# Causal mask by GpSimd selects, diagonal key tiles first, and a re-planned instruction order in a decoder layer on eight cores

## The chip, the cores and the metric

One Trainium2 chip, eight cores, one launch. Each core computes one batch element of the layer; the cores exchange nothing and share the weights in HBM. The time is the device time in microseconds of the slowest core, the median of several runs. Five engines of a core matter here: TensorE (PE, matmuls into PSUM), VectorE (DVE), ScalarE (ACT), GpSimd (POOL, which also issues the DMAs that cast to bf16) and SyncE (SP, which issues the other DMAs). Each runs its own instructions strictly in the order in which the program lists them, and waits at semaphores.

## The reference

```python
h = rmsnorm(x, norm_mix_pre)
proj = h @ w_in                                  # q, k, v, u; 2048 tokens x 1024
q, k = rope(q), rope(k)
y_attn = moba_attention(q, k, v)                 # 8 heads x 64
y_pool = pool_mixer(u, w_pool, b_pool, pool_scale)
x = x + rmsnorm(concat([y_attn, y_pool]) @ w_out, norm_mix_post)
h = rmsnorm(x, norm_ffn_pre)
x = x + rmsnorm(conv_ffn(h, w_up, conv_w, conv_b, w_down), norm_ffn_post)   # D_FF 2816
```

In `moba_attention` a query sees its own block of 256 keys, causally, and the three fully past blocks with the highest gate scores. Inside the own block, scores of keys later than the query are replaced by a very negative number before the softmax; their weights are therefore zero.

## The kernel before

Tokens are cut into 16 tiles of 128 and 4 groups G of 512. The program has three parts.

**Projections.** Tiles of x are loaded, normalised (`prep_norm`: a square with a row sum on ACT or DVE at L619, L620, L629; two small POOL instructions at L604 and L606; a scaling at L635 or L636) and transposed: tiles 0 to 7 by PE (L650), tiles 8 to 15 by a transposing DMA. `vu1` (L769) makes v and u, `qk_unit` (L674) makes q and k of four heads and rotates them on DVE (L681) and POOL (L687, L689); a DMA then moves the halves into place. Weights arrive as float32 in staging slots and are cast by ACT (L551) or DVE (L549). The slots 4 and 5 lie in the same memory as the four x buffers `xs0` to `xs3`, so an x tile can be loaded there only when the weights of that slot have been cast. At the start 88 matmuls on zeros (L491) keep PE running.

**Attention** (`attn(G)`, L818). For each head h and key tile kt up to the group's last, a score matmul puts 128 keys x up to 512 queries into a PSUM bank (L830), ACT takes the exponential into one of eight bf16 buffers `PT` (L844), and for each query tile of 128 a matmul with V (L848, 65 columns, the last one the row sum) adds into the head's bank. The MoBA mask of whole blocks is part of the score matmul (8 extra rows of its 72). The last four key tiles of a group lie on the diagonal; there a second score matmul (L835, identity times a triangle of -30000) adds the causal mask to one 128 x 128 square before the exponential. DVE divides by the row sum (L863, L865). There are three score banks and one bank for the sums, so the sums of the next head wait for the division of this one.

**Output projection and FFN.** `sec1` (L904) multiplies by w_out, with a square (L911), two small POOL instructions, a scaling (L914), the residual add on POOL (L917), a second square, a scaling (L922) and a transposing DMA; tiles 0 to 11 are woven into `attn(2)` and `attn(3)`. `up_section` (L954) and `down` (L1072) are the FFN, twice.

**What sets the order.** Nothing of the order is written by hand. A planner (`Sched.schedule`) plays all instructions through with a cost for each (`cost`, `LAT`, `SLACK`) and a priority (`sc.base`), and lists for each engine the instructions in the order in which they come up; small random amounts (`SEED`, `SHAKE`) are added to the ends, so that another seed gives another order. The waits that the program then contains are true dependencies. What the planner's costs get wrong, an engine pays by waiting in its fixed order.

Of the kernel before, what the change touches and what calls it, by code (L numbers as in the profile page):

```python
# [17 lines left out]
H = 8  # L18
# [3 lines left out]
NEG = -30000.0  # L22
# [3 lines left out]
WARM = 88  # L26
SEED, SHAKE = 923, 0.15
PE_Y = 3
# [41 lines left out]
class Sched:  # L70
# [9 lines left out]
    def __init__(self, nc, st):  # L80
        self.nc = nc
        self.st = st
        self.streams = {e: [] for e in COMPUTE + ("sp",)}
        self.sems = {e: st.enter_context(nc.semaphore("s_" + e)) for e in COMPUTE}
        self.dsem = {}
        self.ops = []
        self.order = 0
        self.base = 0
        self.rng = np.random.default_rng(SEED)

    def _collect(self, eng, rd, wr, wp, deps):
# [11 lines left out]
    def _add(self, o, raw, rd, wr, wp, prio=None):  # L103
        o["shake"] = SHAKE * float(self.rng.random()) if "pe" not in o["alts"] else 0.0
        seen = set()
# [54 lines left out]

    def dma(self, queue, key, pairs, rd=(), wr=(), wp=(), deps=(), nbytes=524288, cast=False, prio=None, turn=False):
        raw = self._collect(queue, rd, wr, wp, deps)
        if key not in self.dsem:
            self.dsem[key] = [self.st.enter_context(self.nc.semaphore("d_" + key)), 0]
        fn = lambda e: [e.dma_start_transpose(out=o_, in_=i_) if turn else e.dma_start(out=o_, in_=i_) for (o_, i_) in pairs]  # L165
        o = dict(kind="dma", key=key, turn=turn, sig=False, seq=0, slack=0.0, ndma=len(pairs), nbytes=nbytes, cast=cast,
                 alts={queue: (fn, (0.62 if queue == "pool" else 0.45) * len(pairs), 0.0)})
        return self._add(o, raw, rd, wr, wp, prio)

    def schedule(self):  # L170
# [26 lines left out]
        while done < len(ops):  # L197
# [15 lines left out]
            t, _, e = best  # L213
# [43 lines left out]
            else:  # L257
                fin = t + o["dur"]
            o["t0"], o["t1"] = t, fin
            fin += o["shake"]  # L260
# [91 lines left out]
def build():  # L352
# [26 lines left out]
    with ExitStack() as st:  # L379
# [124 lines left out]

        def load_x(tt, deps=()):
            s = tt % 4
            dma("sp", "fx%d" % s, [(xs[s], x_d[tt * 128:(tt + 1) * 128, :])], wr=[buf("xs%d" % s)], deps=deps)

# [5 lines left out]
        for tt in range(NT):  # L514
            xsrc[tt] = (xs[tt % 4], buf("xs%d" % (tt % 4)))
        for i in range(3):
# [107 lines left out]
        def prep_norm(tt):  # L624
# [6 lines left out]
            else:  # L631
# [5 lines left out]
                1024, dict(dve="x2", act="sb"), rd=[xab, rb], wr=[xb])  # L637
            if tt == 3:
                scaled.append(xb.w[-1])
# [178 lines left out]
        def attn(G, between=None):  # L818
            nkt = 4 * G + 4
            its = [(h, kt) for h in range(H) for kt in range(nkt)]  # L820
            N = len(its)
# [3 lines left out]
            def qk(n):  # L825
# [4 lines left out]
                last_sc[0:] = [op("pe", lambda e: e.matmul(bk[u.ids[0]][:, c0:512], lhsT=KT[kt // 4][0:72, h, (kt % 4) * 128:(kt % 4) * 128 + 128],  # L830
                                            rhs=QT[G % 2][0:72, h, c0:512], start=True, stop=(nd < 0)),
                   rd=[buf("KT%d_%d" % (kt // 4, h // 4)), buf("QT%d_%d" % (G % 2, h // 4)),
                       buf("QTm%d" % (G % 2)), buf("KTind%d" % (kt // 4))], wr=u.b, n=512 - c0, deps=last_sc[:])]
                if nd >= 0:
                    op("pe", lambda e: e.matmul(bk[u.ids[0]][:, c0:c0 + 128], lhsT=ident, rhs=tri, start=False, stop=True),  # L835
                       rd=[buf("cst")], wp=u.b, n=128)

            qk(0)
            qk(1)
            for n in range(N):  # L840
# [4 lines left out]
                                                                  scale=SCALE),  # L845
                   rd=u.b, wr=[buf("PT%d" % p)], n=512 - c0)
                for qb in range(c0 // 128, 4):
                    op("pe", lambda e, h=h, kt=kt, qb=qb, p=p, pb=pb: e.matmul(  # L848
                        bk[pb.ids[0]][:, qb * 65:qb * 65 + 65], lhsT=PT[p][:, qb * 128:qb * 128 + 128], rhs=VA[:, kt, h, 0:65],
                        start=(kt == 0 and qb == 0), stop=(kt == nkt - 1)),  # L850
                       rd=[buf("PT%d" % p), VA_b[kt], buf("VAones%d" % (kt // 8))], n=64, **W(kt == 0 and qb == 0, pb.b[0]))
                if n + 2 < N:
                    qk(n + 2)
                if kt == nkt - 1 and between is not None:
                    between(h)
                if kt == nkt - 1:
                    r, k = h % 2, (h // 2) % 2
# [254 lines left out]
        def next_x(G):  # L1112
            for tt in range(4 * G, 4 * G + 4):
                load_x(tt, bulk if G < 3 else move1)
            load_rope(G, bulk)
# [33 lines left out]
        lw = buf("ws%d" % wslot[7]).w[-1]  # L1149
        bulk.append(lw)  # L1150
        vu(0, 0)
# [24 lines left out]
        qk_some(1, (("k", 0), ("q", 0), ("k", 1), ("q", 1)))  # L1176
        move1 = union(["QT1_1", "KT1_1"])
        sc.base = P_ATT
        attn(0)
# [85 lines left out]
def host_prep(inputs):  # L1265
# [52 lines left out]
    idtri[:, 0, :] = np.eye(128)  # L1318
    idtri[:, 1, :] = np.where(tp > t, NEG, 0.0)
    c = lambda a: np.ascontiguousarray(a, dtype=f)  # L1320
# [18 lines left out]
```

How the kernel before makes its waits and increments, by code:

```python
            def body(e):  # L322
                waited = {}
                for o in self.streams[eng]:
                    need = {}
                    for d in o["deps"]:
                        k = "d_" + d["key"] if d["kind"] == "dma" else d["eng"]
                        if k not in need or need[k][1] < d["seq"]:
                            need[k] = (d["sem"], d["seq"])
                    for k, (sem, val) in need.items():
                        if waited.get(k, 0) < val:
                            e.wait_ge(sem, val)
                            waited[k] = val
                    ins = o["fn"](e)
                    if o["kind"] == "dma":
                        for i in ins:
                            i.then_inc(o["sem"], 16)
                    elif o["sig"]:
                        ins.then_inc(o["sem"], 1)
```

## Time and profile before

| | |
|---|---|
| median of 3 runs | 779.73 us (776.73, 779.73, 795.33) |
| the profiled execution | 778.17 us, span of its slowest core 776.6 us |
| spans of the eight cores | 768.8 to 776.6 us, mean granted clock 0.988 to 0.995 |
| busy PE, DVE, ACT, POOL | 754.9, 469.2, 387.4, 286.7 us |
| PE waits that the profile names | 14.1 us in 8 waits, the longest 5.9 us |

A span runs from the first to the last instruction of the slowest core; the 1.6 us between it and the execution's time lie around it. "Busy" for PE is modelled and includes the pipeline's latency, so the pace of matmuls is read from their starts. A name in an arrow such as `L848 <- DVE L865` says which line waited and which line's end released it.

### The profile page before, as it was taken

What the parts mean: (1) busy time and instruction counts of PE and PEld (TensorE: products, weight loads), DVE (VectorE), ACT (ScalarE), POOL (GpSimd) and SP (SyncE); (2) the same over time, 40 slices, a digit from 0 to 9 for tenths busy, and PEclk for the clock granted to TensorE, in tenths of its full rate; (3) what the DMA queues carried; (4) which work ended last, traced back from release to release, by engine and by line L of the source; (5) the groups of instructions that cost most, each with busy time, mean ns of one, the idle gap of its engine ahead of it and who ended that gap; (6) DMA issues with size and microseconds to landing.
All of it is one profiled execution on the core that took longest, in us unless ns stands there. A gap on an engine that the chain in (4) does not pass through costs nothing.

```text
span 776.6 us, 14872 instructions; the slowest of 8 cores (768.8 to 776.6 us)
## 1 busy us (share of the span) xinstructions
PE 754.9 (97%) x4866; PEld 385.0 (50%) x4866; DVE 469.2 (60%) x702; ACT 387.4 (50%) x619; POOL 286.7 (37%) x309
## 2 busy tenths in 40 slices
PE   7997999999999999999999999999999999999996
PEld 5644655455655555444444444444444444444443
DVE  4786658654555555578787781322877877772223
ACT  3835567158899999554554440211445454441111
POOL 1273324301455560557655562100343444321000
PEclk9899899999999999999999999999999999999998
DMA  8978589119579565678897676342444444001321
GB/s 256 321 243 199 81 187 198 50 28 144 108 193 215 161 170 131 109 136 160 169 194 122 116 115 102 106 166 108 109 82 82 69 71 79 1 0 57 110 99 62
DMA packets 63067, 99.21 MB, mean 128 GB/s; under 512 B 35856, under 2 KB 41872, under 8 KB 61968
## 3 DMA queue, kind: packets, MB, share of 16 engines
q1 hardware_dynamic: 50304, 65.88, 31.2%
q0 software_dynamic: 12688, 32.38, 25.6%
q8 instruction: 41, 0.67, 0.4%
q14 instruction: 34, 0.28, 0.1%
HBM read 100.60 MB, written 16.78 MB: 151 GB/s over the span
## 4 chain that ended last, share of the span: by engine, by line
PE 90%; DMA 3%; DVE 2%; issue 2%; ACT 1%; POOL 1%; SPq 1%; DVEq 0%; ACTq 0%; POOLq 0%
PE ps L954 38%; PE ps L1072 18%; PE ps L830 7%; PE ps L904 7%; PE ps L769 7%; PE ps L674 5%; PE ps L848 4%; DMA MEM<-x 3%; PE ps L1065 1%; PE ps L835 1%; SPq L165 1%; PE ps L797 1%; ACT MEM L844 0%; PE ps L650 0%; DVE MEM L681 0%
## 5 line engine op out<-in xcount | busy, mean ns | idle before, releaser
L954 PE MATMUL ps<-MEM 128*128 128x512 bf16 x1408 | 309.8, 379 | 1.3 <-DVE MEM L975 1.3
L954 PEld LDWEIGHTS ps<-MEM 128*128 128x128 bf16 x1408 | 136.5, 98 | 164.0 <-issue 2.2
L965 ACT ACTIVATE MEM<-ps,MEM 128x1024 f32<-128x1024 f32 x88 | 105.9, 1203 | 147.2 <-PE ps L954 144.0
L844 ACT ACTIVATE MEM<-ps 128x512 bf16<-128x512 f32 (+1 forms) x320 | 149.4, 541 | 38.7 <-PE ps L835 17.1
L991 POOL TENSOR_TENSOR MEM<-MEM 128x1024 bf16<-128x1024 f32 x44 | 105.2, 2391 | 118.9 <-DVE MEM L978 82.0
L968 DVE SCALAR_TENSOR_TENSOR MEM<-ps,MEM 128x1023 f32<-128x1023 f32 x88 | 112.8, 1282 | 57.9 <-ACT MEM L965 57.7
L1072 PE MATMUL ps<-MEM 128*128 128x512 bf16 x660 | 142.8, 379 | 0.0
L971 DVE SCALAR_TENSOR_TENSOR MEM<-ps,MEM 128x1022 f32<-128x1022 f32 x88 | 112.7, 1281 | 8.2 <-DVE MEM L968 0.5
L1072 PEld LDWEIGHTS ps<-MEM 128*128 128x128 bf16 x660 | 64.4, 98 | 78.0
L830 PE MATMUL ps<-MEM 72*128 72x512 bf16 (+1 forms) x320 | 102.8, 349 | 0.1
L604 POOL TENSOR_SCALAR MEM<-MEM 128x1 f32<-128x1 f32 x63 | 13.7, 218 | 197.7 <-ACT MEM L1077 118.8
L1081 DVE SCALAR_TENSOR_TENSOR MEM<-ps,MEM 128x1024 f32<-128x1024 f32 x15 | 19.3, 1284 | 104.7 <-POOL MEM L606 104.6
L848 PEld LDWEIGHTS ps<-MEM 128*128 128x128 bf16 x1088 | 58.8, 97 | 38.4 <-issue 8.2
L1077 ACT ACTIVATE MEM<-ps 128x1024 f32<-128x1024 f32 x15 | 15.3, 1023 | 123.9 <-PE ps L1072 119.9
L848 PE MATMUL ps<-MEM 128*128 128x65 bf16 x1088 | 69.5, 193 | 6.9 <-DVE MEM L865 6.8
L904 PE MATMUL ps<-MEM 128*128 128x512 bf16 x256 | 72.9, 379 | 0.0
L769 PE MATMUL ps<-MEM 128*128 128x512 bf16 (+1 forms) x320 | 72.2, 350 | 0.1
L674 PE MATMUL ps<-MEM 128*128 128x512 bf16 x256 | 58.2, 379 | 0.0
L165 POOL DMA_DIRECT2D MEM<-w_up_r x44 | 26.1, 594 | 71.4 <-PE ps L954 33.7
L989 ACT ACTIVATE MEM<-MEM 128x1024 f32<-128x1024 f32 x44 | 46.1, 1048 | 4.7 <-DVE MEM L971 3.2
L917 POOL TENSOR_TENSOR MEM<-MEM 128x1024 f32<-128x1024 f32 x16 | 43.2, 2699 | 13.5 <-DVE MEM L914 13.4
L681 DVE TENSOR_TENSOR MEM<-ps,MEM 128x512 f32<-128x512 f32 x64 | 42.4, 685 | 6.6 <-PE ps L674 4.7
(103 smaller groups left out, 620.6 us busy)
## 6 DMA issues: line engine op xcount, KB each, us to landing
MEM<-w_up_r POOLq DMA_DIRECT2D x44, 512.0 KB, 5.5
MEM<-x SPq DMA_DIRECT2D x32, 512.0 KB, 5.5
x1s<-MEM SPq DMA_DIRECT2D x16, 512.0 KB, 5.4
MEM<-x1s SPq DMA_DIRECT2D x16, 512.0 KB, 3.9
out<-MEM SPq DMA_DIRECT2D x15, 512.0 KB, 2.6
MEM<-w_down POOLq DMA_DIRECT2D x22, 256.0 KB, 7.5
MEM<-w_qk SPq DMA_DIRECT2D x4, 1024.0 KB, 20.7
MEM<-MEM SPq DMA_DIRECT2D x24, 128.0 KB, 5.6
```

Of the source, the lines that this page charges most:

```text
L674: mm = op("pe", lambda e, c=c, s=s: e.matmul(bk[bb[s].ids[0]], lhsT=wqk[wi][:, c, s * 128:(s + 1) * 128], rhs=HY[:, c, G * 512:(G + 1) * 5 ...
L769: op("pe", lambda e, c=c, ca=ca, cb=cb: e.matmul(bk[u.ids[0]][:, ca:cb], lhsT=HY[:, c, tt * 128:(tt + 1) * 128], rhs=wvu[s][:, c, ca:cb], ...
L830: last_sc[0:] = [op("pe", lambda e: e.matmul(bk[u.ids[0]][:, c0:512], lhsT=KT[kt // 4][0:72, h, (kt % 4) * 128:(kt % 4) * 128 + 128], rhs= ...
L844: op("act", lambda e, c0=c0, u=u, p=p: e.activation(out=PT[p][:, c0:512], in_=bk[u.ids[0]][:, c0:512], func=AF.Exp, scale=SCALE), rd=u.b, ...
L848: op("pe", lambda e, h=h, kt=kt, qb=qb, p=p, pb=pb: e.matmul(bk[pb.ids[0]][:, qb * 65:qb * 65 + 65], lhsT=PT[p][:, qb * 128:qb * 128 + 128 ...
L904: mm = op("pe", lambda e, c=c, dh=dh: e.matmul(ps(u)[:, dh * 512:(dh + 1) * 512], lhsT=HY[:, c, tt * 128:(tt + 1) * 128], rhs=w_out_sb[:, ...
L954: mm = op("pe", lambda e, c=c, half=half, pr=pr, ws=ws, tb=tb: e.matmul(bk[pr.ids[tb]], lhsT=wu[ws][:, c, half * 128:(half + 1) * 128], rh ...
L965: op("act", lambda e, pr=pr, ch=ch, ts=ts: e.activation(out=tA[ts], in_=ps(pr)[:, :], func=AF.Identity, scale=cwb[:, ch, 2:3], bias=cwb[:, ...
L968: op("dve", lambda e, pr=pr, ch=ch, ts=ts: e.scalar_tensor_tensor(out=tA[ts][:, 1:1024], in0=ps(pr)[:, 0:1023], scalar=cwb[:, ch, 1:2], in ...
L971: op("dve", lambda e, pr=pr, ch=ch, ts=ts: e.scalar_tensor_tensor(out=tA[ts][:, 2:1024], in0=ps(pr)[:, 0:1022], scalar=cwb[:, ch, 0:1], in ...
L991: op("pool", lambda e: e.tensor_tensor(out=gbuf[p], in0=tA[tg], in1=tA[tv], op=ALU.mult), rd=[tA_b[tg], tA_b[tv]], wr=[g_b[p]], deps=alias ...
L1072: op("pe", lambda e, c=c, dh=dh, i=i, p=p: e.matmul(bk[p.ids[dh]], lhsT=gbuf[c][:, i * 128:(i + 1) * 128], rhs=wd[c][:, dh * 512:(dh + 1) ...
```

## The change

Five things are edited.

1. The second score matmul goes. After the exponential of a diagonal tile, POOL sets the 128 x 128 square above the diagonal to zero in `PT` by an `affine_select`. Only the one matmul with V that reads this square waits for POOL (buffer `PM`); the others wait for ACT alone, as before.
2. In a head the four diagonal key tiles come first, then the earlier ones.
3. x tiles 8 to 15 use the x buffers in another rotation (tile 8 goes to `xs2` and not to `xs0`), and their loads no longer wait for the last staged weight (`bulk`).
4. The casts of the first weight wait for the scaling of x tile 1 and not of tile 3.
5. The planner takes x loads to land 3 us later than its costs say, and draws its random amounts from other seeds, twice as large; the second seed begins at `attn(0)`. The constant `tri` is changed on the host, and nothing reads it any more.

```diff
-SEED, SHAKE = 923, 0.15
+SEED, SHAKE = 1348, 0.3
+SEED2, SHAKE2 = 1506, 0.3
+X_LATE = 3.0
...
             else:
                 fin = t + o["dur"]
+            fin += o.get("late", 0.0)
...
-        def load_x(tt, deps=()):
-            s = tt % 4
-            dma("sp", "fx%d" % s, [(xs[s], x_d[tt * 128:(tt + 1) * 128, :])], wr=[buf("xs%d" % s)], deps=deps)
+        def load_x(tt, deps=(), turn=0):
+            s = (tt + turn) % 4
+            dma("sp", "fx%d" % s, [(xs[s], x_d[tt * 128:(tt + 1) * 128, :])], wr=[buf("xs%d" % s)], deps=deps, late=X_LATE)
...
-            if tt == 3:
+            if tt == 1:
                 scaled.append(xb.w[-1])
...
-            its = [(h, kt) for h in range(H) for kt in range(nkt)]
+            kts = list(range(4 * G, nkt)) + list(range(4 * G))
+            its = [(h, kt) for h in range(H) for kt in kts]
...
-                                            rhs=QT[G % 2][0:72, h, c0:512], start=True, stop=(nd < 0)),
+                                            rhs=QT[G % 2][0:72, h, c0:512], start=True, stop=True),
...
-                if nd >= 0:
-                    op("pe", lambda e: e.matmul(bk[u.ids[0]][:, c0:c0 + 128], lhsT=ident, rhs=tri, start=False, stop=True),
-                       rd=[buf("cst")], wp=u.b, n=128)
...
+                nd = kt - 4 * G
+                if nd >= 0:
+                    o = op("pool", None, rd=[buf("PT%d" % p), buf("cst")], wr=[buf("PM%d" % p)])
+                    keep = lambda e, c0=c0, p=p: e.affine_select(out=PT[p][:, c0:c0 + 128], in_=PT[p][:, c0:c0 + 128], pattern=[[1, 128]],
+                                                                 compare_op=ALU.is_ge, fill=0.0, base=0, channel_multiplier=-1)
+                    o["alts"] = dict(pool=(keep, 0.34, 0.38))
                 for qb in range(c0 // 128, 4):
...
-                        start=(kt == 0 and qb == 0), stop=(kt == nkt - 1)),
-                       rd=[buf("PT%d" % p), VA_b[kt], buf("VAones%d" % (kt // 8))], n=64, **W(kt == 0 and qb == 0, pb.b[0]))
+                        start=(kt == kts[0] and qb == 0), stop=(kt == kts[-1] and qb == 3)),
+                       rd=[buf("PT%d" % p), VA_b[kt], buf("VAones%d" % (kt // 8))] + ([buf("PM%d" % p)] if qb == nd else []),
+                       n=64, **W(kt == kts[0] and qb == 0, pb.b[0]))
...
-                load_x(tt, bulk if G < 3 else move1)
+                load_x(tt, bulk if G < 3 else move1, 2)
...
         lw = buf("ws%d" % wslot[7]).w[-1]
-        bulk.append(lw)
...
+        sc.rng, sc.amp = np.random.default_rng(SEED2), SHAKE2
         sc.base = P_ATT
         attn(0)
```

The lines of the changed kernel lie 3 to 9 further down (L165 becomes L168, L491 L495, L650 L654, L769 L773, L830 L835, L844 L846, L848 L856, L865 L874, L917 L926; the select is L852). The order is changed throughout; three places follow.

**SP, after the loads of the staged weights** (w_ut are the last two of them; `x` are tiles 8 to 11, `MEM 32x4x512` the halves of k and q after the rotation, whose wait for `s_pool` is one for the POOL rotation of group 1). Before:

```order
L165 DMA MEM<-w_ut 128x2048 [waits d_ws4,s_act,s_dve]
L165 DMA MEM<-MEM 32x4x512 [waits d_ws0,s_pool]
L165 DMA MEM<-poolc 128x768 [waits d_ws4]
L165 DMA MEM<-x 128x1024 [waits d_ws5,s_act,s_dve]
L165 DMA MEM<-MEM 32x4x512 [waits s_pool]
L165 DMA MEM<-x 128x1024
L165 DMA MEM<-x 128x1024 [waits s_dve,s_act]
L165 DMA MEM<-x 128x1024
```

Now:

```order
L168 DMA MEM<-w_ut 128x2048 [waits d_ws4,s_act,s_dve]
L168 DMA MEM<-x 128x1024 [waits d_ws5,s_act,s_dve]
L168 DMA MEM<-x 128x1024
L168 DMA MEM<-rope 128x1024 [waits d_rp0,s_dve]
L168 DMA MEM<-poolc 128x768 [waits d_ws4]
L168 DMA MEM<-MEM 32x4x512 [waits d_ws0,s_pool]
L168 DMA MEM<-x 128x1024 [waits s_dve,s_act]
L168 DMA MEM<-x 128x1024
```

Tiles 8 and 9 now stand ahead of the first DMA that waits for POOL; tiles 10 and 11 still stand behind it.

**POOL, in `attn(3)`** (small instructions of the norms and the residual adds of `sec1`, whose wait for `s_dve` is the scaling before). Before:

```order
L917 TENSOR_TENSOR MEM<-MEM 128x1024 [waits d_fx1,s_dve]
L604 TENSOR_SCALAR MEM<-MEM 128x1 [waits s_act]
L606 TENSOR_TENSOR MEM<-MEM 128x1 [waits s_pool]
L604 TENSOR_SCALAR MEM<-MEM 128x1 [waits s_dve]
L606 TENSOR_TENSOR MEM<-MEM 128x1 [waits s_pool]
L917 TENSOR_TENSOR MEM<-MEM 128x1024 [waits d_fx2,s_dve]
```

Now:

```order
L926 TENSOR_TENSOR MEM<-MEM 128x1024 [waits d_fx0,s_dve]
L852 AFFINE_SELECT MEM<-MEM 128x128 [waits s_act,s_pe] x4
L608 TENSOR_SCALAR MEM<-MEM 128x1 [waits s_act]
L608 TENSOR_SCALAR MEM<-MEM 128x1 [waits s_dve]
L610 TENSOR_TENSOR MEM<-MEM 128x1 [waits s_pool] x2
L926 TENSOR_TENSOR MEM<-MEM 128x1024 [waits d_fx1,s_dve]
L852 AFFINE_SELECT MEM<-MEM 128x128 [waits s_act,s_pe] x2
```

The four selects of a head stand behind residual adds that wait for DVE and for a load.

**PE, at the start** (L491, now L495, are the matmuls on zeros; L650, now L654, the transposes of x tiles; L769, now L773, the v and u matmuls). Before:

```order
L491 MATMUL ps<-MEM 128x256 x15
L650 MATMUL ps<-MEM 128x128 x8
L491 MATMUL ps<-MEM 128x256 x14
L650 MATMUL ps<-MEM 128x128 x16
L769 MATMUL ps<-MEM 128x256 x48
```

Now:

```order
L654 MATMUL ps<-MEM 128x128 x8
L495 MATMUL ps<-MEM 128x256 x4
L773 MATMUL ps<-MEM 128x256 x3
L495 MATMUL ps<-MEM 128x256
L773 MATMUL ps<-MEM 128x256 x2
L495 MATMUL ps<-MEM 128x256 x2
L773 MATMUL ps<-MEM 128x256 x7
L495 MATMUL ps<-MEM 128x256
L773 MATMUL ps<-MEM 128x256 x4
L495 MATMUL ps<-MEM 128x256 x5
L654 MATMUL ps<-MEM 128x128 x16
L773 MATMUL ps<-MEM 128x256 x48
```

Sixteen of the v and u matmuls now come between the matmuls on zeros, ahead of the transposes of tiles 2 and 3.

## Rows read from the trace of the kernel before

**Rows 1.** The page: span, and section 1, busy us (share of the span) xinstructions:

```profile
span 776.6 us, 14872 instructions; the slowest of 8 cores (768.8 to 776.6 us)
...
PE 754.9 (97%) x4866; PEld 385.0 (50%) x4866; DVE 469.2 (60%) x702; ACT 387.4 (50%) x619; POOL 286.7 (37%) x309
```

**Rows 2.** Stretches: length, busy us PE, PEld, DVE, ACT, POOL, clock, DMA share, GB/s:

```profile
20.60:72.10 51.50, 51.46 (x367) 30.37 (x365) 41.18 (x87) 33.26 (x69) 26.50 (x33) 0.97 0.87 257
72.10:78.10 6.00, 0.06 (x2) 0.05 (x2) 1.74 (x4) 0.00 (x0) 0.19 (x1) 0.77 0.81 204
78.10:82.10 4.00, 4.00 (x27) 2.92 (x28) 2.92 (x6) 3.49 (x7) 2.54 (x4) 0.50 0.18 43
82.10:186.00 103.90, 102.86 (x916) 58.09 (x915) 64.27 (x183) 57.54 (x118) 31.82 (x34) 1.00 0.62 114
186.00:317.00 131.00, 128.90 (x1329) 75.55 (x1325) 69.02 (x97) 118.87 (x240) 58.59 (x70) 1.00 0.70 160
317.00:760.00 443.00, 442.94 (x2053) 200.41 (x2054) 273.11 (x292) 163.25 (x166) 162.90 (x153) 1.00 0.49 102
```

**Rows 3.** Timeline, PE, around 71 us: start, length, instruction:

```profile
71.42 0.22 PE L835 MATMUL ps<-MEM 128*128 128x128 bf16 x1
71.48 0.27 PE L830 MATMUL ps<-MEM 72*128 72x256 bf16 x1
71.59 0.22 PE L835 MATMUL ps<-MEM 128*128 128x128 bf16 x1
```

**Rows 4.** Groups of instructions by shape: count, busy us, mean ns, idle before:

```profile
L844 ACT ACTIVATE MEM<-ps 128x512 bf16<-128x512 f32 x224 | 119.3, 606 | 23.9 <-PE ps L830 10.0 <-PE ps L848 6.7 <-PE ps L835 5.6
...
L835 PE MATMUL ps<-MEM 128*128 128x128 bf16 x128 | 27.8, 221 | 0.0
...
L844 ACT ACTIVATE MEM<-ps 128x128 bf16<-128x128 f32 x32 | 9.1, 284 | 13.7 <-PE ps L835 10.7 <-PE ps L830 2.5
```

**Rows 5.** Timeline, PE, 72 to 82 us: in brackets the idle time before:

```profile
78.08 0.71 PE L848 MATMUL ps<-MEM 128*128 128x65 bf16 x10 [5.94 <-DVE MEM L865]
78.60 2.32 PE L769 MATMUL ps<-MEM 128*128 128x256 bf16 x10
```

**Rows 6.** Timeline, DVE, 65 to 80 us:

```profile
76.36 1.23 DVE L620 SCALAR_TENSOR_TENSOR MEM<-MEM 128x1024 bf16<-128x1024 f32 x1 [6.52 <-DMA MEM<-x]
...
77.51 0.42 DVE L865 TENSOR_TENSOR MEM<-ps,MEM 128x256 bf16<-128x256 f32 x1
```

**Rows 7.** Timeline, SP, 38 to 75 us:

```profile
59.75 0.70 SPq L165 DMA_DIRECT2D MEM<-MEM  x1
...
61.25 0.33 SPq L165 DMA_DIRECT2D MEM<-x  x1
...
62.28 2.00 SPq L165 DMA_DIRECT2D MEM<-x  x3
```

**Rows 8.** Waits of the SP queue, 40 to 70 us: total, times, longest:

```profile
SPq L332 <- POOL MEM L687: 15.6, 2, 15.4
```

**Rows 9.** A stretch of two microseconds, columns as in Rows 2:

```profile
56.00:58.00 2.00, 2.00 (x11) 0.89 (x10) 2.00 (x4) 0.00 (x0) 2.00 (x3) 1.00 0.00 0
```

**Rows 10.** Timeline, PE, 14 to 45 us:

```profile
17.74 1.01 PE L650 MATMUL ps<-MEM 128*128 128x128 bf16 x8 [2.70 <-DVE MEM L635]
...
20.59 7.13 PE L769 MATMUL ps<-MEM 128*128 128x256 bf16 x48
```

**Rows 11.** Timeline, ACT, 38 to 48 us:

```profile
39.70 2.10 ACT L551 ACTIVATE MEM<-MEM 128x256 bf16<-128x256 f32 x5 [1.50 <-DMA MEM<-w_qk]
...
45.64 2.10 ACT L551 ACTIVATE MEM<-MEM 128x256 bf16<-128x256 f32 x5
```

**Rows 12.** One line on POOL, the small factor: duration in ns min/median/max:

```profile
L604 POOL TENSOR_SCALAR MEM<-MEM x63: 181/190/1232, 6.8 to 761.3; 128x1 f32<-128x1 f32 x63
```

**Rows 13.** One line on POOL, the residual add: duration in ns min/median/max:

```profile
L917 POOL TENSOR_TENSOR MEM<-MEM x16: 2347/2378/3266, 202.1 to 384.3; 128x1024 f32<-128x1024 f32 x16
```

**Rows 14.** One line on DVE, both tensors read from SBUF, likewise:

```profile
L922 DVE SCALAR_TENSOR_TENSOR MEM<-MEM x16: 1275/1277/2537, 208.9 to 392.5; 128x1024 bf16<-128x1024 f32 x16
```

More of the change, by code:

```diff
@@ L89, in __init__ @@
         self.rng = np.random.default_rng(SEED)
+        self.amp = SHAKE
     def _collect(self, eng, rd, wr, wp, deps):
@@ L103, in _add @@
     def _add(self, o, raw, rd, wr, wp, prio=None):
-        o["shake"] = SHAKE * float(self.rng.random()) if "pe" not in o["alts"] else 0.0
+        o["shake"] = self.amp * float(self.rng.random()) if "pe" not in o["alts"] else 0.0
         seen = set()
@@ L159, in either, with dma @@
         return o
-    def dma(self, queue, key, pairs, rd=(), wr=(), wp=(), deps=(), nbytes=524288, cast=False, prio=None, turn=False):
+    def dma(self, queue, key, pairs, rd=(), wr=(), wp=(), deps=(), nbytes=524288, cast=False, prio=None, turn=False, late=0.0):
         raw = self._collect(queue, rd, wr, wp, deps)
@@ L165, in dma @@
         fn = lambda e: [e.dma_start_transpose(out=o_, in_=i_) if turn else e.dma_start(out=o_, in_=i_) for (o_, i_) in pairs]
-        o = dict(kind="dma", key=key, turn=turn, sig=False, seq=0, slack=0.0, ndma=len(pairs), nbytes=nbytes, cast=cast,
+        o = dict(kind="dma", key=key, turn=turn, sig=False, seq=0, slack=0.0, late=late, ndma=len(pairs), nbytes=nbytes, cast=cast,
                  alts={queue: (fn, (0.62 if queue == "pool" else 0.45) * len(pairs), 0.0)})
@@ L514, in build @@
         for tt in range(NT):
-            xsrc[tt] = (xs[tt % 4], buf("xs%d" % (tt % 4)))
+            xsrc[tt] = (xs[(tt + 2 * (tt > 7)) % 4], buf("xs%d" % ((tt + 2 * (tt > 7)) % 4)))
         for i in range(3):
@@ L849, in attn @@
                         bk[pb.ids[0]][:, qb * 65:qb * 65 + 65], lhsT=PT[p][:, qb * 128:qb * 128 + 128], rhs=VA[:, kt, h, 0:65],
-                        start=(kt == 0 and qb == 0), stop=(kt == nkt - 1)),
-                       rd=[buf("PT%d" % p), VA_b[kt], buf("VAones%d" % (kt // 8))], n=64, **W(kt == 0 and qb == 0, pb.b[0]))
+                        start=(kt == kts[0] and qb == 0), stop=(kt == kts[-1] and qb == 3)),
+                       rd=[buf("PT%d" % p), VA_b[kt], buf("VAones%d" % (kt // 8))] + ([buf("PM%d" % p)] if qb == nd else []),
+                       n=64, **W(kt == kts[0] and qb == 0, pb.b[0]))
                 if n + 2 < N:
                     qk(n + 2)
-                if kt == nkt - 1 and between is not None:
+                if kt == kts[-1] and between is not None:
                     between(h)
-                if kt == nkt - 1:
+                if kt == kts[-1]:
                     r, k = h % 2, (h // 2) % 2
@@ L1318, in host_prep @@
     idtri[:, 0, :] = np.eye(128)
-    idtri[:, 1, :] = np.where(tp > t, NEG, 0.0)
+    idtri[:, 1, :] = np.where(tp > t, 0.0, 3e38)
     c = lambda a: np.ascontiguousarray(a, dtype=f)
```

## The prediction

> **What bounds the kernel now.** First the page's busy times: PE is busy 754.9 of 776.6 us [rows 1], so time is won only where PE gets less work, a better clock or fewer waits. Second the stretches [rows 2], in which the reader should compare the first two busy numbers with the length. From 317 to 760 us, in the FFN, PE is busy 442.9 of 443.0 us at full clock, and nothing of the change reaches it. From 82 to 186 and from 186 to 317 us, where the attention of the later groups lies, PE misses 1.0 and 2.1 us. The hole is at 72.1 to 78.1 us: 6 us in which PE, ACT and POOL do next to nothing, and behind it 4 us at a granted clock of 0.50, the lower of its two levels, 1.2 GHz.
>
> Third the cause of the hole, from PE backwards. PE waits 5.94 us at L848 for the division L865 of the head before [rows 5]. DVE had not come to that division, because ahead of it in its order stands the square of x tile 8 or 9, which waits 6.52 us for the load of x [rows 6]. That load was issued at 61.25 us or later [rows 7]. SP had stood 15.4 us until then for the rotation on POOL (L687) [rows 8], with the x loads queued behind a small DMA that needs it, while the DMA engines moved nothing between 56 and 58 us [rows 9]. So the hole is an x load issued late, not a shortage of bandwidth.
>
> The sum is made against the profiled execution, 778.2 us, whose slowest span is 776.6 us [rows 1]. It lies 1.6 us below the median of the runs shown, 779.7, which of three values is the middle one.
>
> **The second score matmul.** All 128 go [rows 4]. Their listed 221 ns contain the pipeline; the pace is read from starts: a matmul of 256 columns is followed after 0.11 us, and one L835 of 128 columns after 0.06 [rows 3], so 0.055 us each. 128 x 0.055 = **7.0 us** of PE. Half of them lie in the groups 2 and 3. There ACT is next: between 186 and 317 us it is busy 118.9 of 131 us, PE 128.9 [rows 2]; less 3.5 us PE still has 125.4, so PE stays the bound and the gain passes through. The exponentials also lose a predecessor, which costs or gains nothing, as they are not the bound.
>
> **The hole.** The loads of tiles 8 and 9 now stand ahead of the DMA for which SP waited 15.4 us. They need only the casts of the weights in their memory; the last ACT casts before 50 us end at 47.7 [rows 11]. Issued at about 49 us they have the idle DMA engines of 56 to 58 us [rows 9] and land at about 60, where before the square got its data at 76.4 [rows 6]. The square still stands ahead of the fourth head's division in DVE's order, but its data is then there before the 72.1 us at which PE began to wait. The wait goes, **5.9 us**, and with it the low clock, which followed the idle stretch: 4.0 us at half speed [rows 2], **2.0 us**. What is late next are tiles 10 and 11, still behind POOL; their data is wanted later, by ACT.
>
> **The start.** 16 matmuls of v and u, of 48 that took 7.13 us [rows 10], move ahead of the transposes of tile 2, for which PE waited 2.70 us. At 0.149 us each that is 2.4 us; if the clock then stays up and the other 32 run at 0.11 us, 7.13 - 3.5 = 3.6 us. Against it, weights land when they did: ACT stood 1.50 us for w_qk at 39.7 us [rows 11], and PE cannot pass that by much. DVE is busy 41.2 of the 51.5 us from 20.6 on [rows 2], so it too has little to give. Ends 0 and 3.6; I take **1.5 us**, nearer the lower end because of that wait.
>
> **The selects.** The trace has none. On POOL, one input of one column took 0.190 us (median) [rows 12]; two inputs of 1,024 columns took 2.378 [rows 13], so two of 128 columns about 0.190 + 127 x 2.19/1,023 = 0.46. The select reads one input of 128 columns; between 0.19 and 0.46 I take the middle, 0.33, since neither row is nearer. 128 x 0.33 = 42 us of POOL, which costs nothing by itself: in groups 2 and 3 it adds 21 us to 58.6 of 131 [rows 2]. What it can cost is a wait of PE. The four squares of a head come one after the other, and their matmuls with V now wait for POOL; behind them in PE's order stand the next scores. The cover is the other PE work woven in, L904 and the projections, and the fact that the matmuls of a new head wait for the division of the old one anyway. Lower end 0. Upper end: selects at 0.46 make a head's four 0.52 us late; 32 heads, half of it uncovered, 8 us. I take **2 us**, near the lower end, because PE waited only 2.1 us in 131 with ACT as its supplier [rows 2].
>
> **Diagonal tiles first** makes the last exponential of a head 606 instead of 284 ns [rows 4], 0.32 us later per head. PE's woven-in work hides it; without that cover 32 x 0.32 = 10 us. The planner's assumption on x loads, its seeds and the constant cost nothing of their own; what they move is contained above.
>
> **The sum:** 778.2 - 7.0 - 5.9 - 2.0 - 1.5 + 2.0 = 763.8, so **764 us**, with its own ends 759 (start at 3.6, no new waits: 759.7) and 769 (start at 0, new waits at 6).
>
> **Rivals.** (1) **Selects held up by DVE, 770 us.** For it: on POOL the one-column instruction took up to 1.232 us, 1.04 above its median [rows 12], the residual add up to 3.266 against 2.378 [rows 13], and on DVE the scaling L922 up to 2.537 against 1.277 [rows 14]. If every second head is held once, 16 x 1.04 = 16.6 us, half of it hidden, 8.3 us in place of the 2 in the sum: 770. Against it: the medians lie at the minima, so most instructions are not held. (The Trainium skill, "SBUF — State Buffer", section "Who interferes with whom", has a rule for this: a DVE instruction with two SBUF inputs contends with a GpSimd instruction that reads SBUF, and the second one fully blocks. The long maxima agree with that; no row shows which instruction held which.)
>
> (2) **The hole comes back elsewhere, 772 us.** Tiles 10 and 11 still wait behind POOL, and POOL now has selects ahead of the rotations that free SP. If their squares or transposes stop ACT or SP as tile 8's stopped DVE, the 7.9 us are not won: 771.7. Against it: they have two tiles' work more time than tile 8 had.
>
> (3) **The score matmuls of groups 2 and 3 pay nothing, 767 us**, as ACT, busy 91% there [rows 2], sets the pace after all: the sum less its 3.5 us. This is the way in which the change would not do what it says.
>
> (4) **Slower, 799 us: PE waits behind the residual adds.** In `attn(2)` and `attn(3)` selects stand behind a residual add of 2.38 us [rows 13] that waits in turn for a DVE scaling of about 1.28 [rows 14]: up to 3.66 us for a head, and as there is one bank for the sums, the next head cannot go on. Over 16 heads the 14.4 us won are used up at 0.9 us a head, and the kernel is over 2% slower from 1.9 us a head on, (14.4 + 15.6)/16. At 2.2 us, 60% of the most, it takes 764 + 35 = 799. Against it: before, DVE and ACT waited for these same adds without holding PE, and POOL would be busy only 80 of 131 us.
>
> **How the numbers follow.** Forecast 0.64, rival 1 0.14, rival 2 0.09, rival 3 0.05, rival 4 0.08. A range of 758 to 774 takes in the forecast's ends and rivals 1 to 3, and leaves out rival 4 and a tenth more at the edges. A measurement of this kernel tells about 2% from no change, here 764.1 us. The forecast lies at that bound; its low half and a little more, 0.42, counts as faster by over 2%. Its upper part, 0.22, and rivals 1 to 3, 0.28, make 0.50 within 2%, and rival 4 makes 0.08 slower.
>
> **What the changed profile would show.** PE's stretches without a hole near 70 us, with clock 1.00 from there on; SP's x loads issued before 52 us; 4,738 PE matmuls instead of 4,866; PE waits for L852 of under 3 us in total; POOL busy about 329 us; the FFN's stretch as long as before, some 14 us earlier. I am wrong if PE's waits for POOL exceed 6 us, if a wait for x or for a transposing DMA of x shows on PE, DVE or ACT between 55 and 110 us that reaches PE, or if the first v and u matmuls wait for their weight so long that the 64 end no earlier.

## The result, and the profile after

The changed kernel takes 769.1 us (median of four executions, three of them at 766.6 to 769.6) and the kernel before, on the same chip, 778.8: a ratio of 0.987, 95% interval 0.983 to 0.991. That is 1.3% faster, less than the 2% that the prediction wanted for "faster", and inside its range, 5 us above the forecast of 764. The fourth execution took 830.9 us, with a granted clock of 0.89 to 0.93 on four of its cores, and is left out of the ratio. The profiled execution took 768.6 us, 9.5 less than the one before, where the sum had 14.4.

The page of the changed kernel, as in [rows 1]:

```profile
span 767.1 us, 15225 instructions; the slowest of 8 cores (763.0 to 767.1 us)
...
PE 748.9 (98%) x4738; PEld 378.6 (49%) x4738; DVE 476.5 (62%) x702; ACT 387.2 (50%) x619; POOL 334.9 (44%) x437
```

PE lost its 128 matmuls (4,866 to 4,738) and 6.0 us of busy time, not 7.0 or more. GpSimd is at 334.9 us; 329 were expected. The stretches, with the columns of [rows 2]; the lines of the code have moved by 3 to 9:

```profile
72.10:78.10 6.00, 5.98 (x52) 4.00 (x50) 1.78 (x4) 5.54 (x16) 3.13 (x11) 1.00 0.73 134
78.10:82.10 4.00, 4.00 (x20) 1.77 (x19) 2.61 (x5) 1.06 (x3) 2.60 (x3) 1.00 0.53 52
82.10:167.50 85.40, 84.95 (x766) 47.14 (x764) 60.93 (x177) 52.10 (x108) 43.75 (x78) 1.00 0.67 131
167.50:169.89 2.39, 0.00 (x1) 0.00 (x1) 0.21 (x1) 1.21 (x3) 0.00 (x0) 1.00 1.25 200
169.89:174.00 4.11, 4.11 (x25) 2.02 (x25) 0.42 (x1) 1.68 (x3) 0.07 (x1) 0.58 0.80 136
174.00:186.00 12.00, 12.00 (x109) 6.67 (x108) 2.64 (x7) 8.09 (x18) 2.18 (x9) 1.00 0.08 18
186.00:307.50 121.50, 119.39 (x1171) 67.75 (x1170) 71.98 (x93) 108.15 (x216) 79.86 (x117) 1.00 0.72 158
307.50:750.50 443.00, 443.00 (x2054) 200.84 (x2053) 274.59 (x296) 162.31 (x163) 166.54 (x154) 1.00 0.52 103
```

The hole of [rows 2] at 72.1 us is gone: PE is busy 5.98 of the 6 us, at full clock, and in the next 4 as well. The FFN (last row) is as long as before, 443.0 us, and PE is full in it; it begins 9.5 us earlier. So all of the gain, and all that is missing of it, lies ahead of 307 us. What is missing is seen at once: a **new hole** at 167.50 us, 2.39 us in which PE does nothing, and behind it 4.1 us at a granted clock of 0.58, a mixture of the two levels: 0.50, the lower one, from 170.6 to 174.0 us.

What PE waited for there (timeline of PE; in brackets the idle time before):

```profile
166.91 0.59 PE L773 MATMUL ps<-MEM 128*128 128x512 bf16 x2
169.89 0.39 PE L773 MATMUL ps<-MEM 128*128 128x512 bf16 x1 [2.39 <-issue]
170.12 0.38 PE L835 MATMUL ps<-MEM 72*128 72x512 bf16 x1
```

"issue" means that no semaphore explains the wait. In the program's order this third L773 waits for none: it stands behind two of its kind, with operands ready. The same L773 waits on seven of the eight cores, 0.2 to 2.4 us. Around it the DMA engines are full, with the second half of GpSimd's two casts of w_out, issued here:

```profile
154.97 1.80 POOL L168 DMA_DIRECT2D MEM<-w_out  x2 [2.84 <-PE ps L856]
```

And in those microseconds one packet stands out in the table of DMA queues (queue, kind: packets, MB, share of 16 engines; 166 to 169 us):

```profile
q0 software_dynamic: 236, 0.24, 52.5%
q1 hardware_dynamic: 236, 0.20, 44.8%
q8 instruction: 1, 0.02, 2.8%
```

Queue q8 carries instructions, 41 packets of 16 KB in the whole run. PE's records number some 10,480 (4,738 matmuls, as many weight loads and a thousand waits); if the 41 packets are its program, an instruction takes 64 bytes and a packet holds 256. On the seven cores PE goes on 2.3 to 3.0 us after this packet is seen. That made the theory for the runs below: PE's program arrives in blocks, and here a block came late through queues full of w_out.

The selects, in ns (min/median/max), against the 330 assumed:

```profile
L852 POOL TENSOR_SCALAR_AFFINE_SELECT MEM<-MEM x128: 282/292/1347, 56.3 to 294.3; 128x128 bf16<-128x128 bf16 x128
```

Nobody on PE is named as waiting for them. The loads of x tiles 8 and 9 were issued at 48.7 us, where [rows 7] had 61.25 or later.

### The profile page after: what moved, and what is told of

Read it like the earlier page. It is cut to its first block, busy times and chain, and to the rows that moved or that the text cites. A ratio compares the mean times of both kernels' runs of the same rounds, so it can differ in the third digit from the quotient of the medians.

```text
span 767.1 us, 15225 instructions; the slowest of 8 cores (763.0 to 767.1 us)
## 1 busy us (share of the span) xinstructions
PE 748.9 (98%) x4738; PEld 378.6 (49%) x4738; DVE 476.5 (62%) x702; ACT 387.2 (50%) x619; POOL 334.9 (44%) x437
## 4 chain that ended last, share of the span: by engine, by line
PE 94%; DMA 2%; DVE 1%; issue 1%; ACT 1%; SPq 0%; DVEq 0%; ACTq 0%
PE ps L963 39%; PE ps L1081 19%; PE ps L835 8%; PE ps L913 7%; PE ps L678 7%; PE ps L773 7%; PE ps L856 4%; DMA MEM<-w_vu 2%; PE ps L1074 1%; PE ps L801 1%; SPq L168 0%; ACT MEM L974 0%; DVE MEM L553 0%; PE ps L574 0%; PE ps L654 0%
## 5 line engine op out<-in xcount | busy, mean ns | idle before, releaser
L846 ACT ACTIVATE MEM<-ps 128x512 bf16<-128x512 f32 (+1 forms) x320 | 150.2, 539 | 53.3 <-PE ps L835 36.2
L1000 POOL TENSOR_TENSOR MEM<-MEM 128x1024 bf16<-128x1024 f32 x44 | 107.1, 2435 | 114.4 <-DVE MEM L987 81.1
L835 PE MATMUL ps<-MEM 72*128 72x512 bf16 (+1 forms) x320 | 100.7, 349 | 1.3 <-DVE MEM L895 0.9
L773 PE MATMUL ps<-MEM 128*128 128x512 bf16 (+1 forms) x320 | 72.8, 346 | 4.7 <-issue 2.4
L856 PEld LDWEIGHTS ps<-MEM 128*128 128x128 bf16 x1088 | 58.2, 97 | 34.6 <-issue 1.7
L856 PE MATMUL ps<-MEM 128*128 128x65 bf16 x1088 | 66.7, 193 | 0.1
L852 POOL TENSOR_SCALAR_AFFINE_SELECT MEM<-MEM 128x128 bf16<-128x128 bf16 x128 | 45.3, 375 | 40.5 <-ACT MEM L846 30.0
L168 POOL DMA_DIRECT2D MEM<-w_up_r x44 | 26.1, 594 | 48.7 <-PE ps L963 34.4
```

What stands on the lines that cost most here:

```text
L773: op("pe", lambda e, c=c, ca=ca, cb=cb: e.matmul(bk[u.ids[0]][:, ca:cb], lhsT=HY[:, c, tt * 128:(tt + 1) * 128], rhs=wvu[s][:, c, ca:cb], ...
L846: op("act", lambda e, c0=c0, u=u, p=p: e.activation(out=PT[p][:, c0:512], in_=bk[u.ids[0]][:, c0:512], func=AF.Exp, scale=SCALE), rd=u.b, ...
L856: op("pe", lambda e, h=h, kt=kt, qb=qb, p=p, pb=pb: e.matmul(bk[pb.ids[0]][:, qb * 65:qb * 65 + 65], lhsT=PT[p][:, qb * 128:qb * 128 + 128 ...
L1000: op("pool", lambda e: e.tensor_tensor(out=gbuf[p], in0=tA[tg], in1=tA[tv], op=ALU.mult), rd=[tA_b[tg], tA_b[tv]], wr=[g_b[p]], deps=alias ...
```

## The experiments

Times are against the kernel before in the same session (778.8 to 779.4 us). As the time is that of the slowest of eight cores, and what strikes one core need not strike another, each run is also read on its **undisturbed cores**, those that show none of the large waits. Before, the span of such a core was 768.8 us (the slowest 776.6); after, the least disturbed had 763.0 (the slowest 767.1).

**The second score matmuls back, same order.** The planner sees one instruction as before; it issues two (and the constant `tri` is the triangle of -30000 again):

```diff
+ if nd >= 0:
+     mm = e.matmul(bk[..][:, c0:c0 + 128], lhsT=ident, rhs=tri, start=False, stop=True)
```

> The changed kernel with the selects, and in addition the 128 second score matmuls of 128 columns (identity times the mask) back behind their score matmuls; every instruction else stands in the order of the changed kernel (769.1 us). Theory: each costs the pace read before, 0.055 us, and TensorE is the bound throughout: 769.1 + 7.0 = 776.1. Rival: ScalarE sets the pace in groups 2 and 3, where half of them lie: 769.1 + 3.5 = 772.6.

778.6 us, ratio 0.999 (0.997 to 1.001). The sum seems right, and the reason is not: on core 2 PE stood for 9.17 us at one instruction, without a semaphore:

```profile
230.02 0.25 PE L862 MATMUL ps<-MEM 128*128 128x65 bf16 x3
239.44 0.24 PE L862 MATMUL ps<-MEM 128*128 128x65 bf16 x1 [9.17 <-issue]
```

Three more cores waited there 2.9 to 3.4 us, none at the old place. The four others end at 766.1 to 766.9. From the first score matmul to the end they need 712.4 us (766.5 - 54.1 on core 0), where the changed kernel without such waits needs 708.5 (762.4 - 53.9, from a run below): **3.9 us, not 7.0**. Where the other 3 went shows in the stretch from PE's wait for L812, near 205 us, to its wait for L894, near 303. Undisturbed core without the second matmuls (with 64 more instructions ahead, see below), and with them:

```profile
203.89:302.84 98.95, 97.13 (x943) 54.73 (x944) 59.62 (x75) 89.58 (x179) 67.59 (x97) 1.00 0.80 173
```

```profile
207.82:306.77 98.95, 98.46 (x979) 56.35 (x980) 57.15 (x75) 89.69 (x178) 67.57 (x97) 1.00 0.84 172
```

```profile
L839 PE MATMUL ps<-MEM 128*128 128x128 bf16 x36 | 7.7, 219 | 0.0
```

36 of them ran in it, and it is 98.95 us long either way: PE is busy 98.46 us in place of 97.13, and waits of 1.8 us became 0.5. Behind 205 us their time only filled waits.

**Selects of one column, same order.**

```diff
- e.affine_select(out=PT[p][:, c0:c0 + 128], in_=PT[p][:, c0:c0 + 128], pattern=[[1, 128]], ...
+ e.affine_select(out=PT[p][:, c0:c0 + 1], in_=PT[p][:, c0:c0 + 1], pattern=[[1, 1]], ...
```

> The changed kernel in the same order, with selects of one column in place of 128 (the causal mask is left out but for that column), so GpSimd is busy some 15 us less. Theory: TensorE never waits for a select, so nothing is won: 769 within 1 us, and no wait of TensorE for line 852. Rival: the selects hold the squares of a head up without being named as releaser: 769.1 less the 2 us that the prediction put down for them, or 767.

768.5 us, 0.986 (0.982 to 0.990): the same as the change. But an undisturbed core needs about 707.1 us from the first score matmul to the end (core 0: 762.5 - 54.1 less its wait of 1.3; core 2: 760.1 - 53.3 = 706.8), where it was 708.5. The selects cost 1.4 us, spread over small waits; the rival was nearer. Most of it lies behind 205 us: the stretch from the wait for L812 to that for L894 is 97.8 us long where it was 98.95 (core 0), and from the first of these waits to the end six of the cores take 557.5 to 557.8 us in place of 558.7.

```profile
204.86:302.70 97.84, 96.51 (x943) 54.38 (x944) 59.45 (x75) 89.43 (x179) 61.73 (x97) 1.00 0.87 174
```

So in the stretch in which 36 matmuls less brought nothing, selects of one column brought 1.0 us.

**An eighth of the w_out casts, same order.**

```diff
- [(w_out_sb[:, :, i * 512:(i + 1) * 512], w_out_v[:, :, i * 512:(i + 1) * 512])]
+ [(w_out_sb[:, 0:1, i * 512:(i + 1) * 512], w_out_v[:, 0:1, i * 512:(i + 1) * 512])]
```

> The changed kernel in the same order, with casts of w_out that carry an eighth of its rows (the rest of w_out is left out). Theory: the new hole of TensorE at 167.5 us (2.4 us on the slowest core, 0.2 to 1.8 on six others, always at the same L773 that waits for no semaphore) is a block of TensorE's instructions that comes late through DMA engines filled by these two casts; with an eighth of the bytes no core shows the wait, the clock stays at 1.00 from 160 to 180 us, and the slowest core ends 2 to 4 us earlier: 765 to 767. Rival: the wait is of another kind (ScalarE's projections, the transposing DMAs); then it stays on most cores and the time is 769.

768.2 us, 0.987 (0.982 to 0.992). No core waits at the L773; core 1, from 160 us:

```profile
160.00:180.00 20.00, 20.00 (x219) 12.11 (x216) 8.69 (x36) 16.20 (x36) 3.20 (x12) 1.00 0.07 16
```

PE is full and the DMA share is 0.07. The wait went with the bytes, as the theory wanted; the time did not follow: the slowest core was now core 2, with 3.4 us of waiting for ACT at 25 us and 2.23 us at another instruction, L835 at 240 us, again without a semaphore.

**Counting instructions.** Two for a matmul (weight load and matmul) and one for each semaphore waited for, the L773 is number 2,999 of PE's program and that L835 number 4,534 or 4,535; the matmul that waited 9.17 us in the first experiment is number 4,535 of its own program. 4,535 - 2,999 = 1,536 = 6 x 256, so if one of them begins a block of 256, all three do. The runs with other orders, further below, agree: wherever PE stands for 0.4 us or more without a semaphore, in any trace of this study, it is at number 2,998 or 2,999, at 4,534 or 4,535, or at 5,558, which is 4 x 256 behind 4,534 (by cores whose records are complete). On core 1 of the changed kernel PE enters three blocks at 147.7, 169.9 and 183.8 us by the same count, and instruction packets are seen at 148.3, 172.8 and 186.0, each taken to be the block after; the block that came late was then asked for at 159.9, in the midst of the casts, and its packet is seen at 167.0. (The Trainium skill, "Runtime: NRT & Kernel Launch", section "Instruction fetch mechanics", has the blocks of 256 instructions, fetched while the one before runs, and calls the cost of a boundary mostly hidden. The blocks agree with the count; with full DMA engines the boundary cost up to 9.17 us here, so the measurement decides.)

**More instructions ahead.** If this holds, the place of the wait must move with the count alone. 64 or 32 of the 88 matmuls that warm PE up are cut in two:

```diff
- e.matmul(bk[..][:, 0:256], lhsT=zt[:, 0:128], rhs=zt[:, 0:256], ...)
+ for c in ((0, 128), (128, 256)) if i < 64 else ((0, 256),):
+     mm = e.matmul(bk[..][:, c[0]:c[1]], lhsT=zt[:, 0:128], rhs=zt[:, c[0]:c[1]], ...)
```

> The changed kernel in the same order, but 64 of the 88 matmuls that warm TensorE up are cut into two halves of 128 columns, which puts 128 more instructions (a weight load and a matmul each) ahead of everything else and adds no columns. Theory: TensorE's program comes in blocks of 256 instructions, each fetched when TensorE enters the block before; in the changed kernel the fetch of one block fell into the two w_out casts. Half a block earlier it is asked for at about 153 us, before the casts move bytes: no core waits at the L773 at 167.5 us any more, the block now begins 57 matmuls earlier, at an L806, and the slowest core ends 2 to 3 us earlier, 766 to 767. Rival: the wait belongs to that L773 or its operands: it stays on most cores, 769.

766.4 us, 0.986 (0.983 to 0.989). No core waits at the L773. Six cores end at 761.6 to 762.6; the slowest, core 7, at 766.4, because there a select stood behind two rotations on GpSimd and PE waited for it 1.94 us at 113.9 (1.0 us on a second core): a late select, as in the prediction's first rival, though it was not an instruction held up by DVE that made most of it late.

> As the run with 128 more instructions, with 32 matmuls cut in two, so 64 more. Theory: the fetch is asked for at about 156 us, where the w_out casts begin to move bytes, and is late still; but the wait moves to the first matmul of the shifted block, a matmul with V of 65 columns at about 166 us, 29 matmuls ahead of the L773. Time 768 to 770. Rival: the wait stays at the L773.

765.5 us, 0.985 (0.982 to 0.988), the fastest version of this study; its interval overlaps that of the change, but its slowest cores lay at 763.6 to 766.5 in four executions, those of the change at 765.0 to 768.1 in three. Seven cores show no wait at the boundary. The eighth, core 6, shows it at the instruction foretold, a matmul with V and not the L773:

```profile
165.85 0.34 PE L860 MATMUL ps<-MEM 128*128 128x65 bf16 x4 [1.10 <-issue]
```

The place moves with the count, which no semaphore or operand explains. (On core 1 of the run with 128 more, PE stood 0.71 us at the boundary 6 x 256 further on.) That the fetch would mostly be late was wrong.

**The start as before.**

```diff
- if tt == 1:
+ if tt == 3:
      scaled.append(xb.w[-1])
```

> The changed kernel with the start as before (the first matmuls of v and u wait for the scaling of tile 3, not of tile 1), order planned anew with the same seeds. Theory: the start was put down at 1.5 us: 769.1 + 1.5 = 770.6, and the first projection of q and k begins 1 to 2 us later. Rivals: the whole of the 3.6 us that it could bring, 772.7; or nothing, as the weights land when they did: 769.

771.3 us, 0.993 (0.990 to 0.995): 2.1 more than the change, though the intervals of the two just overlap. The first projection of q and k begins at 31.7 to 33.5 us instead of 29.1 to 32.6. By 50 us, with all other matmuls of the start done alike, PE has started 53.5 matmuls of q and k (median of the eight cores) here, 59.5 in the changed kernel and 56.5 in the kernel before; at 0.22 us each the new start is 1.3 us ahead of this run and 0.7 us ahead of the kernel before.

**The x loads alone, on the kernel before.**

```diff
- xsrc[tt] = (xs[tt % 4], ...)
+ xsrc[tt] = (xs[(tt + 2 * (tt > 7)) % 4], ...)
- bulk.append(lw)
```

> The kernel before with the x loads of the change alone (tiles 8 to 11 go into the other two pairs of buffers and wait no longer for the last weights; the planner adds 3 us to a load); mask, first tiles and seed as before, order planned anew. Theory: the hole at 72 us (5.9 us and 2.0 of low clock) closes, nothing else changes: 778.8 - 7.9 = 771. Rival: the new order opens a wait of the same size elsewhere: 776 to 779.

773.8 us, 0.993 (0.991 to 0.996). The hole is closed on every core (spans 769.7 to 771.7), 5 us won on the profiled executions, not 7.9: core 7, the slowest, came 1.9 us later than core 0 to its first score matmul (61.9 against 60.0), and an undisturbed core gained nothing from the new order (769.7 against 768.8 before).

**The mask alone, on the kernel before.**

```diff
+ o["alts"] = dict(pool=(keep, 0.34, 0.38))
- op("pe", lambda e: e.matmul(bk[..][:, c0:c0 + 128], lhsT=ident, rhs=tri, ...))
```

> The kernel before with the mask part of the change alone (selects on the exponentials, diagonal tiles first, no second score matmul; x loads, start and seed as before), order planned anew. Theory after the runs so far: the second matmuls paid 4.5 us (in groups 0 and 1 alone) and the selects cost 1 to 2: 778.8 - 3 = 776, with the hole near 72 us still there. The prediction's terms: -7.0 + 2.0, 774. Rival: the new order closes the hole by itself: 768.

788.1 us, 1.011 (1.006 to 1.016): **slower**, which no theory had. GpSimd around 72 us on core 3, and what PE did:

```profile
71.61 0.54 POOL L848 TENSOR_SCALAR_AFFINE_SELECT MEM<-MEM 128x128 bf16<-128x128 bf16 x2
76.45 0.19 POOL L604 TENSOR_SCALAR MEM<-MEM 128x1 f32<-128x1 f32 x1 [4.30 <-DVE MEM L620]
76.71 0.54 POOL L848 TENSOR_SCALAR_AFFINE_SELECT MEM<-MEM 128x128 bf16<-128x128 bf16 x2
```

```profile
76.87 0.71 PE L852 MATMUL ps<-MEM 128*128 128x65 bf16 x10 [3.55 <-POOL MEM L604]
```

On four cores the old hole is there, by a shorter way: the small factor L604 of x tile 8 or 9 waits 4.30 us for its square, and two selects stand behind it. On top of it come waits without a semaphore of 3.1 to 5.0 us on four cores near 300 us, at number 5,558 of PE's program. The least disturbed core ends at 769.9 us, against 768.8 before, so in this order the mask won nothing there either.

**The change without its x loads.**

```diff
- xsrc[tt] = (xs[(tt + 2 * (tt > 7)) % 4], ...)
+ xsrc[tt] = (xs[tt % 4], ...)
+ bulk.append(lw)
```

> The changed kernel with the x loads as before (tiles 8 and 9 in the same buffers as before, all behind the last weights, no 3 us on the planner's loads), order planned anew with the same seeds. Theory: the loads of tiles 8 and 9 come late again, and as the selects stand behind the norms of those tiles on GpSimd, TensorE waits at 70 to 80 us for a select: 4 to 8 us with the low clock, 773 to 777. Rival: the new order avoids it: 767 to 770.

791.4 us, 1.015 (1.012 to 1.018). All cores wait 3.0 to 4.7 us at 66 to 69 us, the place expected, but for a DMA and not for a select; four cores wait 4.3 to 10.9 us at 247 to 255 us for another DMA, which nothing here explains.

**Half of the exponentials in groups 2 and 3, same order.**

```diff
+ c1 = 512 if G < 2 else (c0 + 512) // 2
- op("act", lambda e, ...: e.activation(out=PT[p][:, c0:512], ...
+ op("act", lambda e, ...: e.activation(out=PT[p][:, c0:c1], ...
```

> The changed kernel in the same order, with exponentials in groups 2 and 3 that cover half of their columns (the other half of those probabilities is left out and stays stale). ScalarE gets some 40 us less work there, TensorE the same. Theory: ScalarE sets the pace behind 205 us, which is why the second score matmuls cost nothing there; the way from the wait for line 812 at about 205 us to the end, 558.7 us on undisturbed cores, becomes at least 2.5 us shorter, and the time is 765 or less. Rival: TensorE sets the pace there too and the second matmuls are hidden in its own pipeline: 558.7 us stays within 0.5, 769.

769.2 us, 0.988 (0.986 to 0.990). From 200 to 240 us ACT is busy 27.04 us in place of 37.19, and PE 39.48 in place of 39.47:

```profile
200.00:240.00 40.00, 39.48 (x419) 22.92 (x417) 20.27 (x29) 27.04 (x78) 29.52 (x46) 1.00 0.85 187
```

```profile
200.00:240.00 40.00, 39.47 (x417) 23.13 (x416) 20.63 (x29) 37.19 (x77) 28.93 (x45) 1.00 0.86 162
```

From the wait near 205 us to the end an undisturbed core takes 558.4 us (762.8 - 204.4) against 558.7. ACT is not what the matmuls waited for: my theory fell. The rival's numbers came true, but its reason, that PE hides the second matmuls in its own pipeline, does not fit the run with selects of one column, where the same matmuls took 1.0 us less. The longest wait that PE still has there, beside what the selects cost, is for DVE. In the changed kernel, POOL, DVE and PE near 283 us:

```profile
282.16 2.35 POOL L926 TENSOR_TENSOR MEM<-MEM 128x1024 f32<-128x1024 f32 x1
```

```profile
275.01 1.27 DVE L931 SCALAR_TENSOR_TENSOR MEM<-MEM 128x1024 bf16<-128x1024 f32 x1
...
282.22 3.38 DVE L931 SCALAR_TENSOR_TENSOR MEM<-MEM 128x1024 bf16<-128x1024 f32 x1
285.52 0.41 DVE L895 COPY MEM<-ps 128x512 bf16<-128x512 bf16 x1
```

```profile
286.08 0.38 PE L835 MATMUL ps<-MEM 72*128 72x512 bf16 x1 [0.95 <-DVE MEM L895]
```

The scaling L931 takes 3.38 us instead of 1.27 ([rows 14] had one of 2.54) while the residual add L926 runs; the copy L895 stands behind it on DVE, and PE waits 0.95 us for that copy. (By the Trainium skill, "SBUF — State Buffer", section "Who interferes with whom", a DVE instruction with two SBUF inputs contends with a GpSimd instruction that reads SBUF, and the one that issues second is blocked until the first ends. The trace agrees: L931 starts 0.06 us after the add, and ends 1.1 us after it.) With the second matmuls in place PE comes to this point later, and the wait is not there.

**Two other seeds.**

```diff
- SEED, SHAKE = 1348, 0.3
+ SEED, SHAKE = 11, 0.3
- SEED2, SHAKE2 = 1506, 0.3
+ SEED2, SHAKE2 = 12, 0.3
```

> The changed kernel with two other seeds (11 and 12) for the planner's random lateness; nothing else differs than the order. Theory: the order decides by luck which waits and instruction blocks meet which transfers, so another pair is worse than the chosen one by 2 to 10 us: 771 to 779. Rival: the terms alone decide: 767 to 770.

780.4 us, 1.002 (1.000 to 1.003), a little over the expected range: the same work in another order loses all that was won. PE waits here for selects on every core, six times 0.2 to 0.6 us behind 195 us, and 1.7 to 2.1 for an exponential near 274 us; the rest of the 11 us is not named by single waits.

## Why the prediction came out as it did

The range and the class held. The forecast's sum was 5 us too low: one term was mis-sized, one was missing, and the choice of the seeds, put at nothing, can move the time by as much as the whole gain.

- **The second score matmul, -7.0: measured -3.9**, with the selects in place. The price of 0.055 us was about right: ahead of 205 us (groups 0 and 1, and group 2 but for its last head) 92 of them cost 3.9 us, and another 0.8 us vanished in a wait of PE for DVE (L581) at 66 us, together 0.051 each. The step that failed is "so PE stays the bound and the gain passes through". The 36 matmuls behind 205 us were worth 2.0 us and brought nothing, as PE spent the time in waits that it had not had before. Rival 3 said this of groups 2 and 3 and named ACT; the run with half the exponentials shows that it is not ACT. The run with selects of one column shows that 1.0 us of it hangs on the selects; another 0.95 us is the wait for DVE behind the residual add, of which 0.85 is left in that run.
- **The hole, -5.9 and -2.0: place and cause right, the size nearly.** The slowest core before lay 7.8 us above one that had only 0.7 us of it (0.9 of the 7.8 lie ahead of the first score matmul), and after, PE is full there at full clock. The x loads alone closed it on every core, and won 5 us in their order.
- **The start, -1.5: between -0.7 and -2.1**, the lower by the work done at 50 us, the upper by the run without it, in which the order changed too. That the clock stays up came true on four cores, at 1.00 from 20 to 25 us; the others, the slowest among them, had one spell of 3.4 us at 0.50 at the start, and the cores before spells of 3.4 to 6.8 us.
- **The selects, +2.0: +1.4**, at 0.292 us each instead of 0.33, measured without the second matmuls. Waits for a late select, as in rival 1, were seen in one run at 1.0 and 1.9 us, behind rotations on GpSimd. Rival 4 did not occur.
- **Missing: a late block of instructions, +4.1** on the slowest core (2.39 us, and half of the 3.4 us at clock 0.50). Rival 2 had a hole that comes back elsewhere, but at tiles 10 and 11 and by the x loads. The new one has nothing to do with x: in the new order the w_out casts are issued at 155 us, where they met the fetch of a block; before, they were issued at 174 us, and no core shows a wait of this kind of 0.5 us or more.
- **The seeds, of which the prediction says that they "cost nothing of their own".** With another pair the same change takes 780.4 us, 11 more, and is no faster than the kernel before. One other pair was tried, and none on the kernel before; how much of the 9.5 us belongs to the five edits in general, and how much to a lucky order, stays open. That the time lies in the range holds for this pair, and nothing in the forecast told it from others.

-3.9 - 7.9 + 4.1, and 0.7 to 2.1 for the start, make -8.4 to -9.8, against -9.5 measured on the profiled executions. The 1.4 of the selects is not in this sum: the -3.9 was measured with the selects in place and the 1.4 without the second matmuls, and behind 205 us the two are in part the same waits. With the 1.4 added it is -7.0 to -8.4. What selects cost beside the second matmuls no run shows, and terms from runs whose order changed are no better than a microsecond or two.

The signs held: no hole near 70 us, 4,738 matmuls, the loads of x tiles 8 and 9 before 52 us, no wait of PE for L852. Two failed: the FFN's start came 9.5 us earlier and not 14, and behind 70 us the clock was not 1.00 throughout (0.50 for 3.4 us after the late block). And one thing was wrong in the manner of the sum: it treated the parts as independent. Alone, the mask is 1.1% slower and the x loads 0.7% faster; the whole without the x loads is 1.5% slower. In the run with the mask alone the selects stood behind the norms of x on GpSimd and PE waited there, so the earlier loads may be what makes the selects pay; that is argued and not shown, as each of these runs has an order of its own, and an order by itself was worth 11 us.

## What to carry to other kernels

A matmul taken from a full TensorE pays only up to the next wait: look in each stretch for what would be late by a microsecond, and count the gain there as lost. Where a time is that of the slowest of several cores, read a core that nothing disturbed for the work, and the distance of the slowest from it for the accidents; they have different causes. Where a planner's random numbers set the order, try other seeds on both kernels before a gain is put down to an edit: here one pair of seeds took all of it away. In a long program that is written out instruction by instruction, a large transfer can delay the program itself: a wait without a semaphore, at the same instruction on most cores, while the DMA engines are full, can be moved by a few dozen instructions put ahead.

## What the hardware showed that was not expected

PE's program arrives in blocks of 256 instructions through the same DMA engines as the data. Most boundaries show no wait; with those engines full, one cost 0.2 to 2.4 us and another up to 9.17 us, in which DVE did nothing and ACT and POOL 0.4 and 1.5 us of work. In the changed kernel PE went on 2.3 to 3.0 us after the block's packet was seen. Its wait of 2.39 us was followed by 3.4 us at a granted clock of 0.50; the waits of 1.84 us and less at the same place, on other cores, were not. The length of a wait alone does not tell: elsewhere one of 1.60 us (the mask alone, core 2, at 272 us) was followed by 3.4 us at 0.50, and one of 2.23 us (the eighth of w_out, core 2, at 240 us) was not.
